# A decoder layer with 32 experts on one core: gate and up weights in two transfers an expert instead of four

## What is computed

```python
def expert_block(args):
    x_e, e = args
    gu = x_e @ w_gate_up[e] + b_gate_up[e]
    gate = jnp.minimum(gu[:, :D_FF], SWIGLU_LIMIT)
    ...
```

## Time and profile before

| what | value |
|---|---|
| runs | 1449.36, 1450.7, 1454.94 us; median 1450.7 |
| profiled execution | 1452.34 us, its span 1450.6 us |
| PE busy | 1391.4 us (96%) |
| DVE, ACT, POOL busy | 468.4, 285.6, 104.9 us |
| q1 | 477.88 MB, 81.6% of the sixteen engines' span |
| gate-up issues | 128 of 2048 KB, median 20.1 us from issue to landing |
| down issues | 62 of 2048 KB, median 22.2 us; at the end 5 smaller ones (3 of 1024 KB, 2 of 512 KB) |

### The profile page before, as it was taken

How to read it: one execution, slowest core, us unless ns; L and a number is a source line. 1 busy time by engine, 2 the same in 40 slices (tenths; PEclk the granted TensorE clock), 3 DMA queues, 4 the chain that set the end, 5 groups by cost and what they waited for, 6 DMA issues and landing times.

```text
span 1450.6 us, 19691 instructions
## 1 busy us (share of the span) xinstructions
PE 1391.4 (96%) x7350; PEld 615.4 (42%) x7350; DVE 468.4 (32%) x1106; ACT 285.6 (20%) x609; POOL 104.9 (7%) x217
## 2 busy tenths in 40 slices
PE   7999999998999999999999999999999999999987
PEld 3446555766764454333333333333333333333322
DVE  1113475554645462133133122231331321212314
ACT  2003344444542211110101101101100101010002
POOL 1000121633410000000000000000000000000000
PEclk9999999999999989999999999999999999999999
DMA  7334684899887689999999999999999999999996
GB/s 266 116 116 169 236 186 146 282 318 279 307 272 227 275 321 427 428 428 429 429 428 429 428 428 429 429 428 429 428 429 429 428 429 427 429 429 428 429 428 252
DMA packets 75469, 509.47 MB, mean 351 GB/s; under 512 B 19066, under 2 KB 25698, under 8 KB 46082
## 3 DMA queue, kind: packets, MB, share of 16 engines
q1 hardware_dynamic: 61378, 477.88, 81.6%
q0 software_dynamic: 13184, 27.89, 6.2%
q10 hardware_dynamic: 864, 3.15, 0.7%
HBM read 502.29 MB, written 10.62 MB: 354 GB/s over the span
## 4 chain that ended last, share of the span: by engine, by line
PE 71%; DMA 20%; issue 3%; DVE 3%; SPq 2%; ACT 1%; POOL 0%; POOLq 0%; DVEq 0%; ACTq 0%
PE PS L1464 25%; PE PS L1494 11%; DMA arena<-in_w_gate_up 10%; PE PS L1438 6%; PE PS L355 5%; DMA arena<-in_w_down 4%; PE PS L2158 4%; PE PS L1430 4%; DMA arena<-in_cache_cmp_kv 2%; PE PS L1326 2%; PE PS L590 2%; PE PS L364 1%; PE PS L604 1%; DMA arena<-in_cache_diff_k 1%; PE PS L1481 1%
## 5 line engine op out<-in xcount | busy, mean ns | idle before, releaser
L1464 PE MATMUL PS<-arena 128*64 128x512 f32 x2048 | 458.6, 598 | 14.0 <-DMA arena<-in_w_gate_up 12.9
L1464 PEld LDWEIGHTS PS<-arena 128*64 128x64 f32 x2048 | 142.1, 137 | 297.0 <-issue 264.8
L1494 PE MATMUL PS<-arena 128*64 128x512 f32 x1024 | 226.9, 594 | 2.3 <-DMA arena<-in_w_down 2.2
L1920 DVE TENSOR_SCALAR arena<-PS 128x512 f32<-128x512 f32 x32 | 22.1, 692 | 451.1 <-PE PS L1473 450.1
L1494 PEld LDWEIGHTS PS<-arena 128*64 128x64 f32 x1024 | 71.7, 137 | 150.5 <-issue 144.3
L1438 PE MATMUL PS<-arena 128*128 128x512 f32 (+1 forms) x180 | 84.2, 608 | 0.0
L1430 PE MATMUL PS<-arena 128*128 128x512 f32 (+1 forms) x192 | 79.4, 617 | 4.5 <-ACT arena L1630 3.7
L355 PE MATMUL PS<-arena 128*128 128x512 f32 (+1 forms) x192 | 79.4, 575 | 2.6 <-DMA arena<-in_w_in 2.6
L1287 POOL COPY arena<-arena 96x64 bf16 (+1 forms) x34 | 8.1, 240 | 993.0 <-PE PS L1501 947.2
L1841 DVE TENSOR_TENSOR arena<-PS,arena 128x512 f32<-128x512 f32 x32 | 21.8, 688 | 163.9 <-PE PS L1446 161.2
L1615 ACT ACTIVATE arena<-arena 128x512 f32<-128x512 f32 x32 | 20.1, 630 | 272.2 <-DVE arena L1920 272.2
(11 more groups left out here) (291 smaller groups left out, 1276.2 us busy)
## 6 DMA issues: line engine op xcount, KB each, us to landing
arena<-in_w_gate_up SPq DMA_DIRECT2D x128, 2048.0 KB, 20.1
arena<-in_w_down SPq DMA_DIRECT2D x62, 2048.0 KB, 22.2
arena<-in_w_in SPq DMA_DIRECT2D x9, 2048.0 KB, 12.7
arena<-in_cache_diff_k SPq DMA_DIRECT2D x64, 256.0 KB, 6.4
arena<-in_cache_diff_v POOLq DMA_DIRECT2D x64, 256.0 KB, 5.2
arena<-in_cache_cmp_kv POOLq DMA_DIRECT2D x64, 128.0 KB, 5.0
arena<-in_cache_sel_kv SPq DMA_DIRECT2D x64, 128.0 KB, 6.8
arena<-in_w_out SPq DMA_DIRECT2D x1, 4096.0 KB, 14.1
```

Source lines behind the costliest of these rows:

```text
L1464: last = nc.tensor.matmul(bank(2 + role + 2 * u)[64 * h:64 * h + 64], hTm[:, k, BS * u:BS * u + BS], gu_w[:, k, D * role + 512 * h:D * rol ...
L1494: last = nc.tensor.matmul(bank(6 + u)[64 * h:64 * h + 64], aT[u][:, c % 4, 64 * (c // 4):64 * (c // 4) + 64], down_w[u][c // 4][:, c % 4, ...
L1920: st(V.tensor_scalar(g1, bank(2 + 2 * u), LIM, None, ALU.min), g1_ready)
```

## The change

Each expert's gate and up weights come in two transfers of four row blocks, 4 MB each, 32 KB in one piece to a partition. The buffer, the order of the transfers and the down weights are as they were. SP waits once a half, for the value of `e_used` for which it waited at the second or the fourth quarter; PE waits once a half as well, and two semaphores are used instead of four.

```diff
-        gu_in, down_in, IN_BASE = place_in[0:4], (sel_in[0:2], sel_in[2:4]), 64 * PAIRS_OF_SEQ
+        gu_in, down_in, IN_BASE = place_in[0:2], (sel_in[0:2], sel_in[2:4]), 64 * PAIRS_OF_SEQ
...
-            eng.dma_start(gu_w[:, 2 * c:2 * c + 2, :], expert_rows(wgu[e, :, 2 * c:2 * c + 2, :], e)).then_inc(gu_in[c], 16)
+            eng.dma_start(gu_w[:, 4 * c:4 * c + 4, :], expert_rows(wgu[e, :, 4 * c:4 * c + 4, :], e)).then_inc(gu_in[c], 16)
...
-            for c in range(4):
-                sp.wait_ge(e_used, c + 1)
+            for c in range(2):
+                sp.wait_ge(e_used, 2 * c + 2)
                 gate_up_weights(sp, 1, c)
...
-                for c in range(4):
-                    sp.wait_ge(e_used, i * 12 + (c - 7))
+                for c in range(2):
+                    sp.wait_ge(e_used, i * 12 + (2 * c - 6))
                     gate_up_weights(sp, first, c)
...
-                for c in range(4):
-                    sp.wait_ge(e_used, i * 12 + (c - 1))
+                for c in range(2):
+                    sp.wait_ge(e_used, i * 12 + 2 * c)
                     gate_up_weights(sp, second, c)
...
-                    if k % 2 == 0:
-                        pe.wait_ge(gu_in[k // 2], i * 32 + 16 * (u + 1))
+                    if k % 4 == 0:
+                        pe.wait_ge(gu_in[k // 4], i * 32 + 16 * (u + 1))
```

More of the change, by code:

```diff
@@ L1226, in pair_weights @@
                     down_weights(sp, first, 0, h)
-            for c in range(4):
-                sp.wait_ge(e_used, 5 + c)
+            for c in range(2):
+                sp.wait_ge(e_used, 6 + 2 * c)
                 gate_up_weights(sp, 2, c)
@@ L1233, in sync_merge @@
                 down_weights(sp, 2, 0, h)
-            for c in range(4):
-                sp.wait_ge(e_used, 11 + c)
+            for c in range(2):
+                sp.wait_ge(e_used, 12 + 2 * c)
                 gate_up_weights(sp, 3, c)
             def pair_weights_as_freed(i, first, second):
-                for c in range(4):
-                    sp.wait_ge(e_used, i * 12 + (c - 7))
+                for c in range(2):
+                    sp.wait_ge(e_used, i * 12 + (2 * c - 6))
                     gate_up_weights(sp, first, c)
```

## The result

The changed kernel takes 1466.42 us (median of 5 runs, 1457.28 to 1470.55); the kernel before takes 1449.53 us (5 runs, 1449.23 to 1454.94). The ratio is 1.0106, with a 95% interval of 1.0079 to 1.0132: some 15 to 17 us slower, clear of the 0.5%.

What follows compares the result with a forecast made beforehand. The DMA queue was taken as the bound, PE 2.5 us a pair quicker. 7.2 + 1.7 + 4.3 - 5.6 + 4.5 + 1.7 = +13.8 us on 1450.7 gave 1464.5 us, range 1457 to 1472.

Steps and rivals of the forecast that it cites:

- (1): Expert 1's first half, issued into an empty queue, lands at 546.0 us; PE is 5.6 us late.
- (2): Expert 2's first half is issued 5.6 us later, into an empty queue; the queue is 5.8 us late.
- (4): Expert 4's first half lands at 629.2 us instead of 622.0; the queue is 7.2 us late.
- (5): PE's idle time ahead of 546.0 us halves its clock: 1.7 us lost (0 to 3.4), queue 8.9 us late.
- (6): At expert 18, where the order of issue changes, the first half's later issue adds 4.3 us.
- (7): 32 KB pieces save 0.1 us a transfer over 56 transfers behind expert 4, 5.6 us (ends 0 and 12.5).
- (8): At the end PE starts expert 31 one quarter later: 4.5 us, plus 1.7 us (0 to 3.4) for the clock.
- The signs: Expected in the profile after: long waits near 546 and 1412 us, queue gaps near 557, 617, 1020 us, later last landing.
- covered: Rival: late issues at experts 2, 4 and 18 are hidden by overlap, leaving some 5 us, 1456; 6 in 100.
- Faster: Rival: longer pieces pay more than all costs, needing 0.35 us a transfer, 445 GB/s; about 1435 at best; 3 in 100.
- Pieces cut back to 16 KB: Rival: hardware cuts the long pieces up, so they save 0; time 1470, within the range, no chance of its own.
- Slower: Rival: 32 KB pieces go at 419 GB/s (1483), or waits of 2.1 us lower the clock each pass; 9 in 100.

Runs made afterwards that it cites:

- e2: Changed kernel with PE's waits for quarters of the kernel before, quarters issued as late as halves; ratio 1.0046 to the kernel before.
- e5: Kernel before with halves of 4 MB for even experts only, odd experts in quarters; ratio 1.0028 to the kernel before.
- e6: Kernel before with halves of 4 MB for odd experts only, even experts in quarters; ratio 1.0092 to the kernel before.
- e4: Changed kernel with the order of pairs 2 to 8 kept to the end, expert 17's down weights ahead of expert 18's gate-up; ratio 1.0166 to the kernel before.
- e1: Kernel before with quarters issued as before, but PE waiting for two quarters at once; ratio 1.0070 to the kernel before.
- e3: Changed kernel with each half sent as two 2 MB transfers with 16 KB pieces, issue and waits kept; ratio 1.0148 to the kernel before.
- e8: Changed kernel with all even experts and experts 1 and 31 back in quarters; ratio 1.0007 to the kernel before.
- e7: Changed kernel with only experts 1 and 31 back in quarters, on PE too; ratio 1.0018 to the kernel before.

## Why the prediction was right, point by point

The time, 1466.4 us, was forecast at 1464.5 (1457 to 1472). The growth was forecast at 13.8 us; the medians give 16.9 and the traces 18.7. Part of the closeness of the time is luck: the kernel before came out at 1449.5 over five runs, where the forecast started from 1450.7. The mechanism held in every step. Against the 18.7, three sizes left the loss too small (the start by 1.9 us, the saving on long pieces by 1.6, and 1.9 that no step had), and one made it too large (the gap at expert 18, by 0.6).

- *The DMA queue is the bound, and every gap in it is lost.* Held. e2, in which PE keeps its quarters and only the issue is late, loses 7 us. (The prediction counts sixteen slices of the stage; the earlier trace rows has twenty-four at 427 to 429 GB/s, and the last, at 252, is behind them. Nothing hangs on it.)
- *(1) and (2), experts 1 and 2.* The forecast wait of 5.6 us on PE was 6.3, since 4 MB into the empty queue took 13.4 us from issue to landing, not 12.7. The landings of expert 2 are 9.2 us late, forecast 7.5.
- *(3)* Held: no gap stands ahead of expert 3. *(4)* From expert 2 to expert 4 the lateness grows by 1.6 us; forecast 1.4.
- *(5), the clock.* Half speed did come behind the first wait, and its cost on the sixteen records was 5.79 - 3.65 = 2.1 us; forecast 1.7.
- *(6), expert 18.* The lateness grew by 1.7 us from expert 4 to expert 18. Forecast: 4.3 less the saving of 28 transfers at 0.1, 1.5. With the 0.07 measured, 1.7 + 2.0 = 3.7 are the gap's. e5, e6 and e4 tie it to the even experts and to the order, and e1, e2 and e3 to both halves of the change together.
- *(7), long pieces.* The sign and the order of size were right, the size was not: 0.07 us a transfer, not 0.1, so 4 us and not 5.6. The cost per piece, read from two rates rounded to 1 GB/s, was the weakest number of the sum. e3 shows the effect by its removal, with the transfers' size changed as well.
- *(8), the end.* The last down weights landed at 1434.8 us before (1400.5 + 34.3 is the issue and its landing) and PE's last bias product ended 1.4 us behind; after, the last chunk landed at 1433.4 us and PE ended 7.7 us behind. That is 6.3 us, forecast 4.5 + 1.7 = 6.2; the clock's part was 5.56 - 3.65 = 1.9.
- *The sum.* From the marks: 12.5 us of lateness at expert 18, less 2.0 saved behind it, then 6.3 at the end, is 16.8 of the 18.7 us measured. The missing 1.9 us are mostly one landing, that of expert 31's first half, which came 1.5 us later than its place in the queue gives. Eight of the twelve traces have a landing there, or one transfer ahead of it, that is 1.0 to 1.7 us late; before, e4, e6 and e8 have none. e2, e5 and e7, where PE never waits over 2.0 us for gate-up weights, have it too, so it doesn't hang on the long waits; the cause is open.
- *The signs.* Two lay just outside their bounds: the last weights landed 12.4 us later from the mark (7 to 12 forecast), and PE ended 6.3 us more than that (5 to 6). The others held; the period of a pair with waits was 58.46 us (862.68 to 921.14), forecast 58.3.

Of the rivals, "covered" falls with e2 and with the gap at 1005 to 1015 us. "Faster" falls with 431 GB/s against the 445 that it needed; the fixed 2.0 us a transfer that it drew from the Trainium skill ("DMA: Bandwidth & Descriptors", Anatomy of one DMA) is not paid in a full queue: 4.895 us for 2 MB and 9.715 for 4 MB leave 0.07 us for it. "Pieces cut back to 16 KB" falls too: the trace has the gate-up weights in packets of 32 KB. "Slower" had one true part: the waits of 2.0 us in mid-stage do bring the clock down at times. Behind one at 745.77 us the changed kernel shows

```profile
745.00:749.00 4.00, 3.23 (x8) 1.01 (x10) 0.00 (x0) 0.00 (x0) 0.00 (x0) 0.59 0.98 418
```

which delays PE, where it has 2.5 us a pair to spare. It cost the queue nothing: behind this wait and the other of its kind in that trace, at 1324.59 us, the next ten landings are 4.9 and 9.7 us apart, as everywhere in a full queue. (The eleventh behind the second one is the late landing of expert 31.)

## What to carry to other kernels

With a single buffer that is refilled as it is used, the size of a transfer is also the grain at which room is given back and work may start. Ask of a larger one not whether the steady stretches bear it (here they did, and a half took 0.8% less time than two quarters) but what it does where the cover is thin: the first refills, each place where the order of issue changes, and the last buffer before the end. Keep it small there; two experts of 32 made 12 of the 15 us. That large ones elsewhere gain anything over the kernel before, no run here shows.

## What was not expected of the hardware

- 32 KB instead of 16 KB in one piece to a partition, in transfers of 4 MB instead of 2, still took the queue from 428 or 429 to 431 GB/s (4.895 us for 2 MB, 9.715 us for 4 MB; 614.4 ns a packet of 16 KB, 1217.9 ns of 32 KB).
- A wait of 1.9 to 2.1 us on PE for gate-up weights sometimes brings the clock down to half (at 745.77 us), and sometimes not: in the twelve traces 20 of 56 such waits have sixteen records behind them that take over 5 us instead of 3.65. Behind all eleven waits of 4.9 to 6.4 us it fell (the sixteen records took 5.1 to 6.4 us), behind none of the 66 under 1.5 us. The page's clock row, in tenths of a slice of 36 us, doesn't show it at all.
- The work ahead of the experts' stage, the same but for one issue, took 523.2 us in one trace and 511.8 in another, further apart than most effects measured here. Two single profiles compared from their starts show 5 us, from the mark 18.7.
